# A two-layer diffusion step on one core: modulation in quarters, modulation rows through DRAM, router on raw rows

## What is computed

```python
for l in range(DEPTH):                      # 2
    sh1, sc1, ga1, sh2, sc2, ga2 = split(silu(cond) @ mod_w[l] + mod_b[l], 6)
    h = rms_norm(x, norm1_g[l]) * (1 + sc1) + sh1
    if l % 2 == 0:   # short gated conv || spatial gating
        o = even_mixer(h, ...)
    else:            # Fourier mixer || latent attention, 12 heads; q, kv from h @ od_w_in
        o = concat([fourier_mix(..), mla_attend(..)]) @ od_w_out
    x = x + ga1 * o
    h = rms_norm(x, norm2_g[l]) * (1 + sc2) + sh2
    x = x + ga2 * hier_moe(h, ...)          # best of 4 groups, 2 of its 4 experts, 16 experts in all
y = rms_norm(x, final_norm_g)
```

## Time and profile before

| | us |
|---|---|
| median of three runs | 846.28 (845.28 to 849.49) |
| profiled execution, its own time | 847.37 |
| its span, first to last instruction | 845.4 |
| TensorE busy | 724.5 (86%) |
| VectorE busy | 221.1 (26%) |
| ScalarE busy | 154.8 (18%) |
| GpSimd busy | 91.1 (11%) |
| DMA | 210.69 MB, 249 GB/s over the span |

### The profile page before, as it was taken

One profiled execution on the slowest core, in us unless ns is written; L12 is line 12 of the kernel. 1 busy time (PEld: TensorE's weight loads), 2 busy tenths in 40 slices (PEclk: granted clock), 3 DMA queues, 4 the chain that ended last, 5 costly groups with the idle time before them and its releaser, 6 DMA issues.

```text
span 845.4 us, 10068 instructions
## 1 busy us (share of the span) xinstructions
PE 724.5 (86%) x3889; PEld 422.1 (50%) x3890; DVE 221.1 (26%) x501; ACT 154.8 (18%) x324; POOL 91.1 (11%) x144
## 2 busy tenths in 40 slices
PE   3899999899985997799749899899998869999940
PEld 0346666444463663456234554477544746666520
DVE  1111113011251211111170323355324511211216
ACT  2110000100231221121030210355203211221201
POOL 2000000000001121111130200000000012121205
PEclk9999999999976999999969999799999669999985
DMA  9989305767992999999791413903003439989944
GB/s 337 333 215 377 107 1 199 254 244 265 385 412 64 408 422 422 421 404 348 276 391 47 142 65 132 412 4 143 7 1 134 165 135 414 394 309 416 423 177 166
DMA packets 68178, 210.69 MB, mean 249 GB/s; under 512 B 11906, under 2 KB 19074, under 8 KB 55092
## 3 DMA queue, kind: packets, MB, share of 16 engines
q1 hardware_dynamic: 57216, 179.09, 55.0%
q0 software_dynamic: 6048, 17.83, 5.8%
q10 hardware_dynamic: 4884, 13.36, 4.2%
HBM read 199.10 MB, written 15.36 MB: 254 GB/s over the span
## 4 chain that ended last, share of the span: by engine, by line
PE 66%; DMA 17%; issue 9%; DVE 4%; POOL 2%; ACT 1%; SPq 0%; ACTq 0%; POOLq 0%; DVEq 0%
PE ps L1163 10%; PE ps L1093 10%; DMA pool<-in_moe_w 9%; PE ps L1234 7%; PE ps L1190 6%; PE ps L1050 5%; PE ps L1288 4%; DMA pool<-h_rows,of_now 3%; DMA pool<-in_mod_w 3%; PE ps L1221 3%; PE ps L1398 3%; PE ps L1250 2%; PE ps L1370 2%; PE ps L1333 2%; PE ps L1147 2%
## 5 line engine op out<-in xcount | busy, mean ns | idle before, releaser
L1163 PE MATMUL ps<-pool 128*64 128x256 f32 x1280 | 147.3, 388 | 11.5 <-issue 7.3
L1163 PEld LDWEIGHTS ps<-pool 128*64 128x64 f32 x1280 | 105.6, 140 | 58.0 <-issue 23.3
L1093 PE MATMUL ps<-pool,yT 128*128 128x512 f32 x192 | 83.0, 593 | 0.0
L1190 PE MATMUL ps<-pool 128*64 128x512 f32 x320 | 73.1, 597 | 6.5 <-DMA pool<-in_moe_w 3.9
L1050 PE MATMUL ps<-pool,cs 128*32 128x512 f32 x384 | 58.2, 650 | 21.1 <-DMA pool<-in_mod_w 9.0
L1234 PE MATMUL ps<-hT,pool 128*128 128x384 f32 x192 | 62.1, 486 | 0.0
L1093 PEld LDWEIGHTS ps<-pool,yT 128*128 128x128 f32 x192 | 36.4, 190 | 45.5 <-issue 45.4
L403 POOL TENSOR_SCALAR rstd<-ss 128x1 f32<-128x1 f32 x24 | 9.9, 414 | 422.8 <-ACT xn L507 378.3
L1234 PEld LDWEIGHTS ps<-hT,pool 128*128 128x128 f32 x192 | 37.7, 196 | 24.5 <-issue 0.5
L1190 PEld LDWEIGHTS ps<-pool 128*64 128x64 f32 x320 | 24.9, 136 | 41.8 <-issue 39.5
L1050 PEld LDWEIGHTS ps<-pool,cs 128*32 128x32 f32 x384 | 14.8, 116 | 61.0 <-issue 33.9
(11 more groups left out here) (194 smaller groups left out, 792.0 us busy)
## 6 DMA issues: line engine op xcount, KB each, us to landing
pool<-in_moe_w SPq DMA_DIRECT2D x96, 1024.0 KB, 12.4
pool<-in_mod_w SPq DMA_DIRECT2D x20, 2048.0 KB, 12.6
pool<-in_mod_w SPq DMA_DIRECT2D x8, 1024.0 KB, 16.5
pool<-in_ev_w_in SPq DMA_DIRECT2D x6, 1024.0 KB, 10.3
pool<-in_ev_w_in SPq DMA_DIRECT2D x2, 2048.0 KB
pool<-in_ev_w_out SPq DMA_DIRECT2D x2, 2048.0 KB, 14.9
pool<-in_od_w_out SPq DMA_DIRECT2D x2, 2048.0 KB, 9.3
pool<-in_od_w_in SPq DMA_DIRECT2D x2, 1856.0 KB, 11.2
```

Of the source, the lines that this page charges most:

```text
L1093: ins = mm(ps[:, 2 * t + n, :], yT[:, k, t * P:(t + 1) * P], weight(parts[k // 4], 4, D)[:, k % 4, n * 512:n * 512 + 512], start=k == 0, s ...
L1163: ins = mm(ps[m, k, 0:DE], hTe.rearrange("p (c n) -> p c n", c=DC)[:, cc, m], w[e][:, cc, :], start=cc == 0, stop=cc == DC - 1)
L1190: ins = mm(ps[m, 4 + n, :], hidT[:, cc, m], w2[e][:, cc, n * 512:n * 512 + 512], start=cc == 0, stop=cc == 1)
```

## The change

- **Modulation.** A round is loaded as four quarters of 2 MB, each with 8 KB runs and two of the eight contraction chunks (`mod_part`), not as four blocks of 512 columns. Round (0,0) stays first. Quarter (0,1,0) runs inside the value part, and the eleven others of (0,1), (0,2) and (1,0) run between conv groups, one after each of the 12 projections but the first. (1,1) stays behind the experts; (1,2) moves behind the first two query turns.
- **Modulation rows.** But for (0,0), columns and gates no longer come from matmuls: POOL writes `mrow` to a DRAM table `mods`, waits for it, and reads columns, gate rows and the terms of the expert rows back (`put_mods`, `take_columns`, `take_gate`, `take_rows`). Norm gain times (1 + scale) is formed in the row.
- **SP's queue.** The biases move to POOL, in 4 DMAs rather than 16; the 22 constants follow the first 13 loads, where they followed the tenth. The experts' slots of layer 0 are filled in another order.
- **Router.** PE transposes raw `x` inside and behind the projection (`turn_raw`); the scale is folded into the router's weights (`router_weights`), the shift into its bias (`shift_logits`, `shift_spread`), and the root is applied to the logits. There is no second norm evacuation and no `by_tokens`: ACT scales the rows, POOL multiplies and adds the terms (`rows_made`) and writes `h_rows`, which has no row 0.
- **Routing.** The row numbers no longer wait for the gate weights; padding rows are sent out of range in the gather too.
- **Attention.** POOL divides the probabilities, which have two buffers; values of two heads are made together and come out transposed (`pair_values`, `pair_out`), so the turning behind the loop goes. Probabilities of a head are turned one head later.

```diff
+        mods = nc.dram_tensor("mods", (2, 2, 6 * D), F32, kind="Internal").ap()
         y_rows = nc.dram_tensor("y_rows", (2 * T, D), F32, kind="Internal").ap()
-        h_rows = nc.dram_tensor("h_rows", (T + 1, D), F32, kind="Internal").ap()
...
+        def mod_part(l, i, part, at=None, limit=NSLOT):
+            item(f"mod{l}.{i}.{part}", 2, mod_w[l, :, i * 2 * D:(i + 1) * 2 * D].rearrange("(p c) n -> p c n", c=DC)[:, 2 * part:2 * part + 2],
+                 (2, 2 * D), (("mod_mm"), 4 * (3 * l + i) + part + 1), limit, at)
...
+        for part in range(4):
+            mod_part(0, 0, part, 2 * part)
+        in0_item("v", 2048, 512, ("v_mm", 3), 8)
+        in0_half(0, (10, 11, 0))
+        mod_part(0, 1, 0, 6)
+        in0_half(1, (1, 2, 3))
+        in0_item("u", 1536, 512, ("sgu_mm", 4), 4)
+        early_loads = len(loads)
+        for (l, i, part), slot in (((0, 1, 1), 8), ((0, 1, 2), 6), ((0, 1, 3), 8), ((0, 2, 0), 6), ((0, 2, 1), 8), ((0, 2, 2), 6),
+                                   ((0, 2, 3), 10), ((1, 0, 0), 8), ((1, 0, 1), 6), ((1, 0, 2), 10), ((1, 0, 3), 8)):
+            mod_part(l, i, part, slot)
...
+        places = [expert_places(0, (6, 7, 10, 11, 8, 9, 4, 5, 0, 1, 2, 3))]
...
-            for n in range(split):
+            for n in range(early_loads):
                 load(n)
-                if n == 7:
-                    biases()
-                if n == 9:
-                    constants()
+            constants()
+            for n in range(early_loads, split):
+                load(n)
...
-                                             bounds_check=T, oob_is_err=False).then_inc(S(f"L{l}_gathered"), 16)
+                                             bounds_check=T - 1, oob_is_err=False).then_inc(S(f"L{l}_gathered"), 16)
...
+            def put_mods(l, i):
+
+                gps.wait_ge(S("mod_row"), 3 * l + i + 1)
+                for r in range(2):
+                    gps.dma_start(mods[l, r, i * 2 * D:(i + 1) * 2 * D].rearrange("(j n) -> j n", j=4), mrow[l][r::32, i, :]) \
+                        .then_inc(S("mods_out"), 16)
+                gps.wait_ge(S("mods_out"), 32 * (3 * l + i))
+
+            def take_columns(l, i, vs):
+
+                for v in vs:
+                    for r in range(2):
+                        gps.dma_start(modcol[l][:, i, v, r, :], mods[l, r, (2 * i + v) * D:(2 * i + v + 1) * D].rearrange("(p c) -> p c", c=DC)) \
+                            .then_inc(S(f"columns{l}{i}"), 16)
...
+            def rows_made(l):
+
+                for t in range(TILES):
+                    root("norm", 3 * (2 * l + 1) + t + 1, t, D)
+                    gps.wait_ge(*L(l, "scaled", t + 1))
+                    if t == 0:
+                        gps.wait_ge(S("h_terms"), 64 * (l + 1))
+                    r = cond_of(t)
+                    ch.link(nc.gpsimd.tensor_tensor(xn[:, t, :], xn[:, t, :], hrow[:, 0, r, :], ALU.mult))
+                    ch.link(nc.gpsimd.tensor_tensor(xn[:, t, :], xn[:, t, :], hrow[:, 1, r, :], ALU.add))
+                    gps.dma_start(h_rows[t * P:(t + 1) * P, :], xn[:, t, :]).then_inc(S("h_rows"), 16)
...
+            gps.wait_ge(S("mod_cmm"), 1)
+            gain_rows(0)
             for t in range(TILES):
                 root("v", t + 1, 3 + t, 512)
-            for t in range(TILES):
-                root("norm", TILES + t + 1, t, D)
+            put_mods(0, 1)
+            take_gate(0, 0)
+            take_columns(0, 1, (1,))
...
+            take_rows(0)
+            rows_made(0)
+            gps.wait_ge(S("x1"), TILES)
+            take_gate(0, 1)
             rows_moved(0)
+            put_mods(1, 1)
...
+            for h in range(NH):
+                gps.wait_ge(S("pinv"), h + 1)
+                for t in range(TILES):
+                    ins = nc.gpsimd.tensor_scalar(probs(h, t), probs(h, t), pinv[:, h % 2, t:t + 1], None, ALU.mult)
+                ins.then_inc(S("probs_even"), 1)
+                if h == 5:
+                    put_mods(1, 2)
+                    take_columns(1, 2, (0,))
...
+            def router_in(l):
+
+                for t in range(TILES):
+                    squares("norm", ("x1", 3 * l + t + 1), xn[:, t, :], x[:, t, :], ss[:, t:t + 1])
+                    act.wait_ge(*L(l, "raw_tr", t + 1))
+                    n = DC if t < TILES - 1 else DC // 2
+                    a_.activation(hT[:, 0:n, t * P:(t + 1) * P], raw_banks(t)[:, 0:n * P].rearrange("p (c n) -> p c n", c=n), ACT.Copy) \
+                        .then_inc(S("raw_T"), 1)
+                    act.wait_ge(*L(2 * l + 1, "norm_root", t + 1))
+                    a_.activation(xn[:, t, :], x[:, t, :], ACT.Copy, scale=rstd[:, t:t + 1]).then_inc(S("scaled"), 1)
...
+            def router_weights(l):
+
+                dve.wait_ge(S(f"columns{l}2"), 32)
+                for r in range(2):
+                    ins = v_.tensor_tensor(wrs[:, r], wr[:, l], modcol[l][:, 2, 0, r, :].unsqueeze(2).broadcast_to((P, DC, NG + NE)), ALU.mult)
+                ins.then_inc(S("rbias"), 1)
...
             def project_out(l):

-                dve.wait_ge(*L(2 * l + 0, "gate_rows", 4))
+                dve.wait_ge(*L(l, "bias_mm", 1))
+                v_.tensor_copy(shifts[0:2, :], ps[0:2, 6, 0:NG + NE]).then_inc(S("rbias"), 1)
+                dve.wait_ge(S("gate"), 32 * (2 * l + 1))
                 for t in range(TILES):
                     for n in range(2):
-                        if (l, t, n) == (0, 1, 1):
-                            mod_round(0, 2)
                         dve.wait_ge(*L(l, "out_mm", 2 * t + n + 1))
                         half = slice(n * 512, n * 512 + 512)
                         link(v_.tensor_tensor(xn[:, t, half], ps[:, 2 * t + n, :], ga[:, cond_of(t), half], ALU.mult))
                         ins = v_.tensor_tensor(x[:, t, half], x[:, t, half], xn[:, t, half], ALU.add)
+                        if (t, n) == (0, 0):
+                            router_biases(l)
                     ins.then_inc(S("x1"), 1)
+                    if t:
+                        logits(l, t - 1)
+
+            def logits(l, t):
+
+                dve.wait_ge(*L(2 * l + 1, "norm_root", t + 1))
+                dve.wait_ge(*L(l, "router_mm", t + 1))
+                link(v_.scalar_tensor_tensor(R["logits"][:, t], router_out(t), rstd[:, t:t + 1],
+                                             rbias[:, cond_of(t), :], ALU.mult, ALU.add))
...
-                link(v_.tensor_scalar(again, found, float(T), float(T), ALU.is_gt, ALU.mult))
-                v_.scalar_tensor_tensor(of_rows[:, :], found, 1.0, again, ALU.max, ALU.subtract).then_inc(S("sources"), 1)
+                v_.tensor_scalar(again, found, float(T), float(T), ALU.is_gt, ALU.mult)
                 link(v_.tensor_scalar(none, found, 0.0, FAR, ALU.is_equal, ALU.mult))
+                link(v_.tensor_tensor(again, none, again, ALU.subtract))
+                v_.scalar_tensor_tensor(of_rows[:, :], found, -1.0, again, ALU.add, ALU.add).then_inc(S("sources"), 1)
+                v_.tensor_tensor(rhs[:, :, 1], steps_now, R["weights"].unsqueeze(3).broadcast_to(bs), ALU.mult).then_inc(S("onehot"), 1)
...
+            def head_sums(h):

                 dve.wait_ge(S("probs"), h + 1)
-                if h:
-                    dve.wait_ge(S("o_out"), h)
-                v_.reciprocal(pinv, psum_of[:, h % 2])
+                if h >= 2:
+                    dve.wait_ge(S("probs_even"), h - 1)
+                v_.reciprocal(pinv[:, h % 2], psum_of[:, h % 2]).then_inc(S("pinv"), 1)
...
+            def pair_out(g):
+                dve.wait_ge(S("o_mm"), g + 1)
+                v_.tensor_copy(yT[:, 2 + g, :], ps[:, 1, 0:T]).then_inc(S("o_out"), 1)
...
+            def mod_part(l, i, part):
+
+                k = 3 * l + i
+                if part == 0 and k:
+                    pe.wait_ge(S("mod_row"), k)
+                name = f"mod{l}.{i}.{part}"
+                arrived(pe, name)
+                w = weight(name, 2, 2 * D)
+                for c in range(2):
+                    for j in range(4):
+                        ins = mm(ps[32 * j:32 * j + 32, 7, :], cs32[:, 2 * part + c, :], w[:, c, j * 512:(j + 1) * 512],
+                                 start=part + c == 0, stop=part + c == 4)
+                ins.then_inc(S("mod_mm"), 1)
...
+            def shift_logits(l):
+
+                pe.wait_ge(S(f"columns{l}1"), 32)
+                for cc in range(DC):
+                    ins = mm(ps[0:2, 6, 0:NG + NE], modcol[l][:, 1, 1, :, cc], wr[:, l, cc, :], start=cc == 0, stop=cc == DC - 1)
+                ins.then_inc(S("bias_mm"), 1)
...
+                        if (t, n) == (0, 0):
+                            shift_spread(l)
+                        if (t, n) == (1, 0):
+                            pe.wait_ge(*L(l, "rbias", 3))
+                            turn_raw(l, 0)
+                        if (t, n) == (1, 1):
+                            router(l, 0)
+                        if (t, n) == (2, 0):
```

(58 more changed lines are left out.)

549 lines of the change are left out of this document (262 added, 287 removed).

## The result

| | before | after |
|---|---|---|
| median, 6 runs each | 846.74 us (845.28 to 849.50) | 841.47 us (840.29 to 843.64) |
| after over before | | 0.9932, 95% interval 0.9903 to 0.9961 |
| profiled execution: its time, span | 847.37, 845.4 us | 841.42, 839.6 us |
| mean granted clock of TensorE | 0.929 | 0.908 |

What follows compares the result with a forecast made beforehand. It took TensorE, 66% of the chain, as the bound. Terms of -12.9 us up to the experts and -6.6 behind summed to -19.5, from the median of 846.28 to 827 us; range 812 to 843.

Steps and rivals of the forecast that it cites:

- Start: First modulation round: four 2 MB loads with 8 KB runs move faster, value part starts at 34.3 us: -6.7 us.
- The late quarter: Quarter (0,1,1), between conv groups: queued behind 13 loads and 22 constants, lands at 75 us, wanted at 69.4: +5.5 us.
- Groups and quarters: Value part and conv groups: twelve quarters' matmuls now stand where TensorE had no gap, 3 x 7.11: +21.3 us.
- Before the projection, in it, the tails: Modulation block before layer 0's projection goes, -13.4; second round leaves that projection, -5.1; tails before experts, -14.5 and -3.2 us.
- eight shift matmuls: Ahead of layer 0's projection: eight new 20-column matmuls for the shifts add 2.4 us; the same again in layer 1.
- GpSimd's hold on VectorE: Tails before the experts: VectorE operations with two SBUF inputs wait for POOL's wide ones: +2.7 us (0 to 6).
- The table's trip: Before layer 0's projection: DRAM write plus read of modulation rows, 11.6 us, hidden under 25.2 us.
- Experts: Expert stages: gathers send padding out of bounds, moving fewer bytes: -3.6 us in layer 0, -2 in layer 1.
- Behind layer 0's experts: Leaving layer 0: no wait for columns, but POOL's sums stand behind two DMAs: nothing net, 3 us either way.
- Attention and layer 1's projection: Layer 1: head pairs at 10.4 us, turning behind the loop goes, shift matmuls and raw turning come: +2.2 us together.
- End: From the last expert matmul to the kernel's end: no change forecast, 0 us.
- POOL dear: Rival: POOL operations hold DVE in full, attention scalings run slower, gathers gain nothing: 843 us, chance 0.20.

Runs made afterwards that it cites:

- e2: Changed kernel with both loads of x moved from ScalarE's queue to the head of SyncE's row: 840.86 us.
- e12: Changed kernel with GpSimd's two wide operations for each layer's third token tile cut to 8 columns: 835.97 us.
- e8: Changed kernel with the gather's padding rows back in range, each fetching row 1 again: 841.33 us.
- e1: Changed kernel with the 22 constant transfers issued by SyncE after its seventh load instead of after the last early load: 835.5 us, ratio 0.988.
- e6: Changed kernel with the 22 constant transfers issued by GpSimd at 27 us, after the roots of x, instead of by SyncE: 835.5 us.
- e9: Changed kernel with the 22 constant transfers issued by GpSimd at 66 us, after the roots of the value part, instead of by SyncE: 840.1 us.

## Why the prediction was wrong, step by step

**Start: -6.7 forecast, -2.0 measured.** The rate was right: 402 GB/s over the 20 us where 381 stood before, against the 400 reckoned with. The landing was not: e2, with x out of the way, shows the last quarter at 29.7 where the sum had 27.3. By then 10.7 MB had moved, and not the 10.0 of the sum: weights of the value part were moving beside it. The rest was x. It used to land at 14.7, beside loads of 2 KB rows, and now landed at 22.0, beside quarters of 8 KB rows (that the rows are the reason is not tested), so the transposes fell to 25 to 30 us, ran at the lower clock and stood in front of two quarters that could otherwise have been done one by one. The prediction never asked when x would land.

**The late quarter: +5.5 forecast, 8.8 measured, against a value part 4.8 us later than forecast.** This is the step that failed most. The quarter was put at 75 and came at 82.0. SyncE was through its loads at 52.3, not 47. The sum put the 22.5 MB of loads and tokens at 56 us, which is 400 GB/s from time zero: it left out the 2.3 us until data flow that the start had reckoned with, and data then flowed at 383 GB/s up to 52.3, at 348 where the loads have 1 KB rows. By 52.3 19.2 MB had moved, so SyncE was 3.3 MB ahead and not 3.8. (SyncE also stood 3.3 us for the slot of (0,1,0), but e2, where that slot comes free 2.4 us sooner, is through at 52.7, so this did not count.) The constants took 22.3 instead of 20.6, the landing 7.4, near the 7 of the sum. The wait then brought 1.5 us of low clock, which had been put at nothing. The quarter's landing, 7.0 us late, with this clock and the 3 us of the next paragraph, puts the conv groups' end at 157.5, some 11 us later than the 146 of the forecast. The late start is not among them: the landing sets that end, and e2 shows that a value part 2.4 us earlier only lengthens the wait. Had the start come as forecast, nothing would have been gained by it. The Trainium skill, "DMA: Bandwidth & Descriptors", Specifications, puts line rate at 512 B and more; 348 at 1 KB, 381 at 2 KB and 402 to 421 at 8 KB differ by a fifth, and the rows decide.

**Groups and quarters: +21.3 forecast, about 24 measured.** Beside a quarter a conv group takes 5.37 us instead of 5.16, and a quarter 1.85 instead of 1.78. Ten such groups and twelve quarters are 3 us. For the switch itself no run was made. A sum over matmuls of equal kinds missed the change of kind.

**Before the projection, in it, the tails: right.** -13.4, -5.1, -14.5 and -3.2 against -15.0, -5.6, -15.6 and -4.4. The 2.4 us for eight shift matmuls were 0.56. GpSimd's hold on VectorE, taken as 2.7, was 3.2 (e12), at the operations that were named. The table's trip was hidden.

**Experts: -3.6 and -2 against -1.3 and -2.5.** The gathers save 2.5 and 1.6 (e8). In layer 0 something else costs 1.2, in layer 1 something else gains 0.9; the order in which the expert buffers are filled changed too, and I did not test it. Behind layer 0's experts, "nothing net, 3 either way" was -2.5: VectorE has one tile done by 413.2 while GpSimd waits for its table, and then waits 4.0 us for GpSimd's sums.

**Attention and layer 1's projection: +2.2 forecast, +5.7 measured.** 10.67 a pair instead of 10.4, where before had 10.52. GpSimd's scaling is 3.04 us a head and not 2.1: a 384-column scaling takes 1.24 us, and 2.34 per 1024 columns did not carry over. It is hidden in the loop, which was said, and not behind it, which was not asked: there its 3.05 us stand between the last softmax and the turning that TensorE waits to do. That is 1.1 us of scaling and 4.0 of lower clock, 2.2 up to the projection and 1.8 in its first 16 matmuls, which had been put at nothing; with 1.4 for five pairs they are more than the 3.5 missed, because the eight shift matmuls took 0.56 us and not 2.4 and the table write at head 5, put at 1, is hidden. The lower clock at the start of the attention (3.8 us against e1) is no part of it, since before had it too, from 530 to 540 us.

**End: 0 forecast, +3.9 measured.** Nothing in the rows of before pointed to it, since the views leave the drain out. 3.6 of it lie behind the last VectorE operation (6.7 us instead of 3.1), where the drain now outlasts the output.

That the time lies inside 812 to 843 is luck in part: the range was made of other terms than those that were missed, the late quarter apart. The chances were too sure of a large gain. The rival "POOL dear" at 843 is nearest in time, but not in mechanism: gathers gained, the hold on VectorE was 0.5 us from what was reckoned, and the dearer scaling (3.04 us for 2.1) is hidden in the loop.

## What to carry to other kernels

A load at the front of a full queue is late by its own issue and by that of everything ahead of it; before crediting an earlier start, find the next landing that does not move with it, since a gain ahead of a fixed landing is only a longer wait. Many small transfers are best kept out of the stretch in which large ones are asked for just in time: here 22 of them cost 2 to 9 us in front of, between or beside the weights, and 22 us on the engine whose own work stood behind them. An engine whose work is hidden inside a loop should be looked at again at the loop's last turn.

## What was not expected of the hardware

- GpSimd's closing drain grows with the software transfers issued in the whole kernel, by 0.082 us each between 42 and 102 of them in the seven kernels on that line, whenever they landed.
- The same four transfers of 0.5 KB landed in 2.4 us from SyncE with nearly idle DMA engines (after), and from GpSimd in 6 us at 40 us (e6) and in 15.7 to 17.3 us at 78 us, with quarters moving beside them (e9).
- Where the attention began at the lower clock, GpSimd's last scaling was followed by some 10 us more of it in nine of ten executions, and VectorE's, which spares 2.1 us, in none of four. Executions of one kernel differ by 6 us in this way.
